# Attention of the second layer starts between the query projection's jobs; block compression moves behind the query with its operands swapped, and its branch is added last

## The reference, cut to what matters

```python
kv = (rmsnorm(h, kv_norm_g) @ w_kv).reshape(B, T, 3, 2, 4, 64)
# branch 0: compressed blocks of 32 tokens, stride 16: 15 blocks per group
flat = blocks(kv[..., 0]) + pos                       # 2048 per block
k_cmp = rmsnorm(gelu(flat_k @ w1_k) @ w2_k, k_norm_g[0])
v_cmp = gelu(flat_v @ w1_v) @ w2_v
# branches 1 and 2: selected and window; with 256 tokens both see all causal tokens
q = rmsnorm((xn @ w_in)[..., :1024] as 16 heads of 64, q_norm_g) * 64 ** -0.5
gates = sigmoid((xn @ w_in)[..., 1024:])              # 3 per head
p_i = masked_softmax(q @ k_i + bias_i)                # for each branch i
o = gates[0] * p_cmp @ v_cmp + gates[1] * p_slc @ v_slc + gates[2] * p_win @ v_win
h = h + o @ w_out
```

## Time and profile before

| | us |
|---|---|
| median of 3 runs (1441.76 to 1444.31) | 1443.74 |
| the profiled execution, its own time | 1440.81 |
| its span, first to last instruction | 1439.2 |
| query jobs 1 to 3 and their sums, compression (from 397.96 to 438) | 40 |
| attention loop to the first output job at full pace (from 438.42 to 507.10) | 69 |
| experts (from 546.35 to the end) | 893 |

### The profile page before, as it was taken

One profiled execution on the slowest core, in us unless ns is written; L12 is line 12 of the kernel. 1 busy time (PEld: TensorE's weight loads), 2 busy tenths in 40 slices (PEclk: granted clock), 3 DMA queues, 4 the chain that ended last, 5 costly groups with the idle time before them and its releaser, 6 DMA issues.

```text
span 1439.2 us, 36218 instructions
## 1 busy us (share of the span) xinstructions
PE 1380.9 (96%) x16208; PEld 831.3 (58%) x16208; DVE 433.9 (30%) x646; ACT 307.4 (21%) x495; POOL 144.5 (10%) x215
## 2 busy tenths in 40 slices
PE   7999999999997799999999999999999999999995
PEld 7999999998895583343343343343343343344343
DVE  5985555555567730110110110110110110110120
ACT  5744543434545821000000000000000000000000
POOL 0600100001203705001001001001001001001001
PEclk9999999999997998999999999999999999999998
DMA  9853465557986056999999999999999999999993
GB/s 280 261 168 118 152 202 176 177 189 166 215 242 240 1 206 252 402 418 402 419 418 400 419 418 401 419 418 402 418 418 401 418 419 402 419 418 390 419 399 143
DMA packets 132786, 454.83 MB, mean 316 GB/s; under 512 B 12452, under 2 KB 74109, under 8 KB 132643
## 3 DMA queue, kind: packets, MB, share of 16 engines
q1 hardware_dynamic: 126386, 435.11, 78.0%
q0 software_dynamic: 6080, 17.37, 5.2%
q10 hardware_dynamic: 176, 0.14, 0.0%
HBM read 436.46 MB, written 14.55 MB: 313 GB/s over the span
## 4 chain that ended last, share of the span: by engine, by line
PE 86%; DMA 8%; DVE 3%; ACT 2%; issue 1%; POOL 0%; SPq 0%; POOLq 0%; ACTq 0%; DVEq 0%
PE ps L1647 85%; DMA more<-in_moe_w_gu 4%; DMA ring<-in_moe_w_down 3%; ACT x_hi L926 1%; DMA ring<-in_a_w_in 1%; DVE arena L1492 1%; DVE arena L1489 1%; DMA arena<-item_rows,arena 0%; ACT arena L1134 0%; PE ps L1951 0%; ACT x_hi L956 0%; DVE arena L1493 0%; ACT between L1155 0%; POOL arena L788 0%; PE ps L1759 0%
## 5 line engine op out<-in xcount | busy, mean ns | idle before, releaser
L1647 PE MATMUL ps<-more,arena 128*32 128x448 f32 x3456 | 330.0, 539 | 4.7 <-DMA more<-in_moe_w_gu 4.7
L1616 DVE TENSOR_TENSOR arena<-arena,ps 128x448 f32<-128x448 f32 x48 | 29.8, 621 | 769.6 <-PE ps L1647 765.4
L1647 PE MATMUL ps<-ring,arena 128*32 128x448 f32 x2688 | 258.7, 542 | 1.2 <-ACT arena L1201 1.2
L1647 PEld LDWEIGHTS ps<-more,arena 128*32 128x32 f32 x3456 | 105.1, 110 | 225.4 <-issue 212.1
L1647 PE MATMUL ps<-ring,between 128*32 128x256 f32 x3360 | 189.6, 379 | 0.5 <-DMA ring<-in_moe_w_down 0.4
L1647 PEld LDWEIGHTS ps<-ring,arena 128*32 128x32 f32 x2688 | 82.2, 110 | 168.3 <-issue 158.2
L522 DVE TENSOR_TENSOR w_lo<-ring,w_hi 128x2048 fp32r<-128x2048 f32 x67 | 153.5, 2294 | 77.8 <-ACT w_hi L516 77.7
L1647 PEld LDWEIGHTS ps<-ring,between 128*32 128x32 f32 x3360 | 105.2, 110 | 86.9 <-issue 7.8
L516 ACT ACTIVATE w_hi<-ring 128x2048 fp32r<-128x2048 f32 x67 | 127.6, 1910 | 97.5 <-PE ps L1647 87.9
L1647 PE MATMUL ps<-more,between 128*32 128x256 f32 x2016 | 115.3, 379 | 0.0
L1212 ACT ACTIVATE arena<-ps 128x448 f32<-128x448 f32 x48 | 26.1, 543 | 414.2 <-PE ps L1647 414.2
(11 more groups left out here) (269 smaller groups left out, 1137.0 us busy)
## 6 DMA issues: line engine op xcount, KB each, us to landing
more<-in_moe_w_gu SPq DMA_DIRECT2D x144, 896.0 KB, 20.0
ring<-in_moe_w_gu SPq DMA_DIRECT2D x112, 896.0 KB, 19.5
ring<-in_moe_w_down SPq DMA_DIRECT2D x80, 896.0 KB, 20.0
more<-in_moe_w_down SPq DMA_DIRECT2D x48, 896.0 KB, 20.2
ring<-in_ffn_w_gu SPq DMA_DIRECT2D x22, 1024.0 KB, 5.1
ring<-in_a_w_in SPq DMA_DIRECT2D x16, 1024.0 KB, 11.6
ring<-in_ffn_w_down SPq DMA_DIRECT2D x11, 1024.0 KB, 5.0
ring<-in_w_kv SPq DMA_DIRECT2D x6, 1024.0 KB, 4.9
```

The lines of the kernel that those rows point to most:

```text
L1616: dve.tensor_tensor(SU[:, a, :], SU[:, a, :], ps[:, b, 0:QUARTER], ALU.mult).then_inc(bank_free[b], 1)
L1647: return pe.matmul(o, w, x, start=start, stop=stop, **kw)
```

## The change

PE's order. Query jobs alternate between banks 2 and 3; the sum of squares of job 0 stands ahead of job 2, that of job 1 and the scores of units 0 and 1 ahead of job 3, then the sum of job 2, the scores of units 2 and 3, the sum of job 3. Only then comes the compression. It is one job `hid` now: the 60 blocks are stationary, the 256 weight columns move, keys land in partitions 0 to 59 and values in 64 to 123. Its gelu is written to `GB` (zeroed by POOL at its front), PE transposes it (`blocks_turned`, job `hidT`, in step 6 of the loop), ACT copies it (`blocks_spread`), and `kc`, `vc`, `kcsum` follow in steps 6 and 8.

```diff
     for b in range(4):
-        job(("qB", b))
+        job(("qB", b), 2 + b % 2)
...
-        CMP_AT = [2 + HB // 2 * ORDER.index(tt) for tt in range(TT)]
+        CMP_AT = [10 + HB // 2 * ORDER.index(tt) for tt in range(TT)]
+        SPLIT_AT = (12, 15, 18)
...
             pool.memset(KCZ, 0.0).then_inc(keys_zero, 1)
+            pool.wait_ge(keys_zero, 1)
+            pool.wait_ge(squares_added, 2)
+            pool.memset(GB, 0.0).then_inc(hid_zero, 1)
+            pool.wait_ge(hid_zero, 1)
...
+            query_squares(0)
+            refill(make_hi, act, ("qB", 0))
+            query_squares(1)
+            query_factors(0)
+            query_squares(2)
+            query_factors(1)
             for s in range(len(units) + LAG):
...
-                if s == 0:
+                if s == 1:
+                    query_squares(3)
+                    query_factors(2)
+                if s == 2:
+                    query_factors(3)
+                if s == 4:
+                    blocks_gelu()
+                if s == 6:
+                    blocks_spread()
+                if s == 7:
+                    block_keys()
+                if s == 8:
                     k = filled(act, ("kcsum",))
...
+                if s in SPLIT_AT:
+                    refill(make_hi, act, ("qB", 1 + SPLIT_AT.index(s)))
...
-            query_scaled(0)
-            refill(make_lo, dve, ("qB", 0))
+            dve.wait_ge(shifted, 16 * 8)
             for s in range(2):
-                dve.wait_ge(shifted, 16 * 8)
                 for g in range(G):
...
-            for n in range(3):
-                refill(make_lo, dve, ("qB", n + 1))
-                biased(n)
...
-                if s == 1:
+                if s == 9:
                     dve.wait_ge(rs_b, 7)
...
-                if s == 4:
+                if s == 8:
                     k = filled(dve, ("vc",))
...
+                if s in SPLIT_AT:
+                    refill(make_lo, dve, ("qB", 1 + SPLIT_AT.index(s)))
                 if s in CMP_AT:
                     cmp_scores(CMP_AT.index(s))
...
+                for k in range(CMP // 4):
+                    for s in range(2):
+                        last = mm(ps[64 * s:64 * s + G * NCMP, b, 0:HID], RC[:, s, CMP // 4 * half + k, :], w[s][:, k, :],
+                                  half == 0 and k == 0, half == 1 and k == CMP // 4 - 1, skip_group_check=True)
...
+                for j in range(4):
+                    last = mm(ps[:, b, P * j:P * j + P], VCZ[:, first // 2 + j, :], PCT[:, tt, first // 8, :], False, True, skip_group_check=True)
```

## The result

The changed kernel takes 1468.99 us (1467.35 to 1470.34, four runs) beside 1442.82 of the kernel before (1441.76 to 1444.31, the three runs above and one more). In three of the experiments a single run took over 2000 us beside others that agree within 1%; it is left out of their medians. The ratio is 1.018, with a 95% interval of 1.0163 to 1.0198: slower by some 26 us. The sign was forecast, the size was not. The sum said +13.2, and 1468.99 lies 5 us above the upper end of the range.

The account below looks back on a forecast made before the run. PE was taken to bound the stretch ahead of the loop, DVE's pace the loop from about unit 4. An end 11.9 us later plus 1.3 for the clock gave +13.2 on 1443.7: 1457, range 1448 to 1464 (8 in 10).

Parts of the forecast that it names:

- part 1: Query stage up to unit 4: despite 6 us of PE idle, unit 4 starts at 438.4, 11.8 us earlier.
- part 2: Units 4 to 12: waits between DVE, ACT and PE added; unit 12 starts at 463.6, 5.5 us earlier than before.
- part 3: Three weight splits in steps 12, 15, 18: 5.1 us each on DVE, 15.3 in all; unit 20 10.4 later.
- cheap splits: Rival, chance 0.14: each split in the loop costs DVE only its own 2.25 us; end 1.9 earlier, 1441.8.
- the nearest row: Values' group in the earlier profile, 16 passes in 1.09 us, used to price the new compression at 8.5 us.
- full overlap: Lower bound for the new compression on PE, its column halves fully overlapping: 7.7 us.
- The rival of the copies landing early: Query stage, chance 0.10: POOL's shifted copies come by 398, PE's pause vanishes, 6 us shorter there: 1451.
- Part 4: Unit 20 to the output job: 0.6 for unit 22's scores and 0.9 for compressed products added; 11.9 later.
- its sentence on activity: On PE's clock: the default state is the throttled one and activity releases it; the trace was said to agree.
- the clock term: Slow PE products in the loop, around the turning in step 20: 1.3 us added, from nothing to 5.
- a low clock to 1463: Rival, chance 0.13: PE stays at 1.2 GHz and becomes the bound from unit 13 to 24, +6 us, 1463.
- no overlap to 1464: Rival, chance 0.08: the new compression's halves do not overlap, 15.4 us in place of 8.5, +6.9, 1464.

## Why the prediction went wrong, point by point

The mechanism of the splits was right, and the sum left out what stands around it. The first step that failed is the start of the new compression in part 1: it waits 3.76 us for its bank, which the forecast had at nothing. The second is the term of part 2 for PE's work ahead of unit 8, 2.3 at full clock, which measured 6.0. The third is that a split in part 3 costs nothing in the steps behind it; there 4.0 more were lost.

**What bounds.** The reading that DVE's queue sets the loop's pace was right. That the splits decide the sign was not: with all three in idle time and the rest as it was, the kernel still takes 9 us more than before (ratio 1.0064), where the forecast's cheap splits had come out 1.9 us faster. Before the loop they had not been free either: without them units 0 to 3 took 2.1 less.

**Part 1.** The PE pause (6 forecast, 5.3 measured) and unit 0 (421.6 against 423.29, less 1.8 for the shift before the diff) held. Unit 3 held too: 434.3 against 436.10 less 1.8. The new compression took 8.8 for 8.5, but by luck: behind the pause the granted clock was 0.83 from 434 to 444. With the clock at 1.00 it took 7.12, less than the 7.7 that I had called full overlap, so the nearest row was too slow by 1.4. The step that failed is the one that let it begin at 428.8 "behind the scores of units 2 and 3, and sum 3". It asked what PE does before it and not who must empty its bank. The kernel gives it bank 6; I had not looked up that bank's last reader. Price: 4.4 up to unit 4 (21.2 against 16.8), and 5.5 by the run with the other banks. The rival of the copies landing early had the right place: the lead was 8.4 longer than it needed to be, though the additions' place in DVE's queue was the lever, not the copies' landing.

**Part 2.** 28.6 from unit 4 to 12 against 25.2. All waits that were forecast are there. DVE waits 2.56 for L1154 (2.2 forecast), 2.56 and 2.14 around `VCZ` (1.1 forecast), 1.38 before `KCZ` (1.5). The term that was too small is the middle one: 2.3 in the sum, 6.0 measured (2.56, 1.29 of work and 2.14). It was reckoned with PE's durations at full clock. The granted clock was 0.52 from 454 to 460, and `vc` takes 1.81, the values 1.98 and the scores 1.59, where the earlier trace rows have 1.09 and 1.13 for the last two.

**Part 3.** The mechanism was right to a tenth: 2.96 idle and 2.29 of work (not the 2.25 that I took from the earlier trace rows), 5.25 for 5.1. The sum was 31.1 and became 35.1. Missing is what a split does to the step behind: its weights are late, so ACT's scaling, ACT's copy of the transposes, PE's transposes and values are late one behind the other, and the next scores stand behind all of them on PE, with `block_values` and the low clock on top. That is the 4.09 before unit 18. It is 1.83 with PE kept busy, and 1.86 without the split at step 15; the values take 1.09 in both. So some 2.2 of it goes with the slow products, which come behind the split's pause. I wrote "in the loop slow products have slack from DVE". They have it only as long as nothing on their way waits for DVE. Three splits cost 17 us measured alone, not 15.3.

**Part 4.** +3.3 instead of +1.5; the scores of unit 22 wait 1.9 (0.6 forecast) and those of unit 30 0.9.

**The clock.** I put 1.3 on it, from nothing to 5, as a term of its own. In the traces it is not one: it lengthens each PE step that is in the chain, so it sat in the misses of parts 2, 3 and 4. How much it was in all is not measured. The run with PE kept busy took 3.6 us less by the marks of units 16 to 18 and 20 to 31, but its whole time is not clear of no change. On the other hand, a low clock where PE is not the last to arrive cost nothing: in the run with ten added matmuls the clock was 1.00 over 8 us in which it had been 0.50, with no gain. The Trainium skill (TensorE: Matmul & The Clock Gate, Terms) puts the penalty at about the throttled time multiplied by (1 - K/N), where K/N is the granted share of the clock; by that I estimate 4 us there. The products themselves agree: `vc` takes 1.01 for 1.81, the values 1.09 for 1.98, the scores of unit 8 1.13 for 1.97. The time of the stretch does not: 0.7 was added, about the 0.8 by which the added work held ACT up, since PE's products were not what was waited for last.

The forecast called an agreement on both halves of its sentence on activity. Those rows show only the fall. The release stands a little later in the same trace: with PE fully busy all the while the clock was 0.50 from 350 to 352, 0.96 from 352 to 354, and 1.00 from 354 to 356.

**The table loads.** In the changed kernel the load of 1.28 starts as the exponentials end and the gelu starts at once behind it (447.23 and 448.52), as the forecast took it from the earlier trace rows; no drain stands beside it. Leaving out both loads and the gelu shortened units 4 to 8 by 2.2.

**The sum.** Unit 0 to 4: +4.4. Unit 4 to 12: +3.4. Unit 12 to 20: +4.0. Behind: +1.8. The lead: -0.2. Less 1.3 for the clock term: 12.1, beside the 13 that separate 26 from 13.2. The range's upper end held one mishap at a time (a low clock to 1463, no overlap to 1464); several small ones in a row were outside of it. The four that cost time had the same sign because each was something left out.

## What to carry to other kernels

When a step is moved into a loop of engines that wait for each other, price it in two parts: its own time, and the place of what it waits for in the other engine's queue, both at the places where the two queues are idle. Here the same six instructions cost 17 us more in one place than in another. Splitting their cost into wait and work does not end it: what the step delays in the third engine's queue came on top. Before saying when a product can start, look up who last reads the bank that it writes; and read each PE duration in a chain behind a pause at the low clock. Test repairs together as well as alone, since the one can use up the idle time that made the other cheap.

## What the hardware showed that I had not expected

Each float32 matmul that the program calls stands as two instructions in the trace. With 128 rows and 512 columns these took 0.45 each at full clock (5.42 for twelve), 0.9 a call. Two calls on the two halves of the rows, as for the scores of a pair of units, took 1.13 together.

The start of the second layer's stages varies by 3.8 us from kernel to kernel with no edit before it (331.6 to 335.4 at the same row), more than 0.2% of the time. A length between marks repeats far better where DVE's queue sets it: units 12 to 16 took 18.06 in the changed kernel, and 18.06 to 18.08 in the four experiments on it that left them alone and in the one on the kernel before. Where PE's clock goes up and down it repeats less well: units 20 to 31 took 17.8, 19.2, 19.2 and 19.3 in the changed kernel and in three kernels with no edit in that stretch.
